# The first of three additions of a pair's weight sums, by accumulating transfers on GpSimd's queue

## The reference

```python
x = x + 0.5 * swiglu(rmsnorm(x, ffn1_norm), ffn1_w_gate, ffn1_w_up, ffn1_w_down)   # hidden width 5632
u = rmsnorm(x, mix_norm) @ w_in                                                     # 2048 x 6144
a = differential attention (4 heads) ; b = stick-breaking attention (8 heads)
x = x + concat(a, b) @ w_out
x = x + 0.5 * swiglu(rmsnorm(x, ffn2_norm), ffn2_w_gate, ffn2_w_up, ffn2_w_down)
x = rmsnorm(x, final_norm)

def swiglu(x, w_gate, w_up, w_down):
    return (silu(x @ w_gate) * (x @ w_up)) @ w_down
```

## Time and profile before

| | us |
|---|---|
| median of 3 runs | 1814.16 (1814.14 to 1814.62) |
| span of the profiled execution | 1811.7 |
| TensorE matmuls busy (8296) | 1800.1, 99% of the span |
| VectorE busy (1715 instructions) | 1415.1, 78% |
| ScalarE busy | 963.3, 53% |
| GpSimd busy | 21.7, 1% |
| HBM read | 346.85 MB, 193 GB/s over the span |

### The profile page before, as it was taken

One profiled execution on the slowest core, in us unless ns is written; L12 is line 12 of the kernel. 1 busy time (PEld: TensorE's weight loads), 2 busy tenths in 40 slices (PEclk: granted clock), 3 DMA queues, 4 the chain that ended last, 5 costly groups with the idle time before them and its releaser, 6 DMA issues.

```text
span 1811.7 us, 22258 instructions
## 1 busy us (share of the span) xinstructions
PE 1800.1 (99%) x8296; PEld 1498.7 (83%) x8296; DVE 1415.1 (78%) x1715; ACT 963.3 (53%) x1210; POOL 21.7 (1%) x19
## 2 busy tenths in 40 slices
PE   9999999999999999999999999999999999999998
PEld 7888888888888888888888888888888888888887
DVE  7889888889898868666666566889888887678865
ACT  7555445555454545555656455555455555345554
POOL 0000000000000000100000000000000000000000
PEclk9999999999999999999999999999999999999999
DMA  9565655556666657655465466665655557566653
GB/s 338 202 218 200 215 192 193 200 199 201 215 212 225 223 172 243 197 174 171 154 195 162 159 225 223 201 219 197 218 188 194 202 197 259 189 204 225 219 171 114
DMA packets 234116, 367.02 MB, mean 203 GB/s; under 512 B 16560, under 2 KB 95152, under 8 KB 234032
## 3 DMA queue, kind: packets, MB, share of 16 engines
q1 hardware_dynamic: 233120, 364.44, 59.4%
q10 hardware_dynamic: 912, 1.48, 0.2%
HBM read 346.85 MB, written 2.10 MB: 193 GB/s over the span
## 4 chain that ended last, share of the span: by engine, by line
PE 99%; DVE 0%; issue 0%; POOL 0%; DVEq 0%; ACT 0%
PE psum L1934 72%; PE psum L1975 14%; PE psum L1847 7%; PE psum L1852 3%; PE psum L1956 1%; PE psum L1808 0%; PE psum L2124 0%; PE psum L2135 0%; PE psum L2150 0%; PE psum L2170 0%; DVE x_res L1796 0%; PE psum L1814 0%; PE psum L1812 0%; PE psum L1813 0%; PE psum L1906 0%; PE psum L2183 0%
## 5 line engine op out<-in xcount | busy, mean ns | idle before, releaser
L1934 PE MATMUL psum<-w_split,x_split 128*128 128x512 f32 x3792 | 872.9, 390 | 0.0
L1934 PEld LDWEIGHTS psum<-w_split,x_split 128*128 128x128 f32 x3792 | 710.0, 188 | 149.7 <-DVE w_split L1252 1.4
L755 ACT ACTIVATE w_split<-w_raw 128x1024 fp32r<-128x1024 f32 (+1 forms) x520 | 517.9, 1013 | 458.2 <-PE psum L1934 325.8
L1252 DVE TENSOR_TENSOR w_split<-w_raw,w_split 128x1024 fp32r<-128x1024 f32 (+1 forms) x520 | 586.2, 1163 | 95.1 <-ACT w_split L755 89.7
L1934 PE MATMUL psum<-w_split,h_split 128*128 128x512 f32 x1920 | 439.2, 389 | 0.0
L1934 PEld LDWEIGHTS psum<-w_split,h_split 128*128 128x128 f32 x1920 | 359.8, 188 | 75.7 <-DVE w_split L1252 1.4
L1102 DVE TENSOR_TENSOR w_split<-w_raw,w_split 128x1024 fp32r<-128x1024 f32 (+1 forms) x244 | 284.0, 1190 | 94.1 <-ACT w_split L643 92.4
L643 ACT ACTIVATE w_split<-w_raw 128x1024 fp32r<-128x1024 f32 (+1 forms) x244 | 247.1, 1032 | 207.4 <-PE psum L1934 158.4
L1975 PE MATMUL psum<-w_split,pair_sums 128*128 128x512 f32 x624 | 162.6, 389 | 0.0
L1975 PEld LDWEIGHTS psum<-w_split,pair_sums 128*128 128x128 f32 x624 | 117.1, 188 | 24.3
L1975 PE MATMUL psum<-w_split,x_split 128*128 128x512 f32 x360 | 94.7, 389 | 0.0
(11 more groups left out here) (240 smaller groups left out, 1051.0 us busy)
## 6 DMA issues: line engine op xcount, KB each, us to landing
w_raw<-in_ffn_up SPq DMA_DIRECT2D x67, 1024.0 KB, 5.4
w_raw<-in_ffn_gate SPq DMA_DIRECT2D x66, 1024.0 KB, 8.0
w_raw<-in_ffn_down SPq DMA_DIRECT2D x64, 1024.0 KB, 5.7
w_raw<-in_w_in SPq DMA_DIRECT2D x48, 512.0 KB, 4.8
w_raw<-in_w_in SPq DMA_DIRECT2D x24, 1024.0 KB, 5.3
w_raw<-in_ffn_gate SPq DMA_DIRECT2D x42, 512.0 KB, 5.8
w_raw<-in_ffn_up SPq DMA_DIRECT2D x40, 512.0 KB, 6.2
w_raw<-in_w_out SPq DMA_DIRECT2D x16, 1024.0 KB, 5.1
```

Of the source, the lines that this page charges most:

```text
L755: nc.scalar.activation(w_split[:, n % 2, 0, part[0]:part[1]], w_raw[:, slot, part[0]:part[1]], ACT.Copy).then_inc(hi_made, 1)
L1252: nc.vector.tensor_tensor(w_split[:, n % 2, 1, part], w_raw[:, slot, part], w_split[:, n % 2, 0, part].bitcast(F32), ALU.subtract).then_in ...
L1934: ins = mm(psum[:, bank + t, :], x[:, a, t * P:(t + 1) * P], w[:, b, k, :], start=kk == from_ and (a, b) == (0, 0) and t in begins, stop=k ...
```

## The change

VectorE's first add of each pair (L1260, 128x1024) is dropped. In its place GpSimd's queue issues, as soon as the low part of the pair's block job is made, one DMA transfer with `accum_op=ALU.add` of 512 KB: it reads the second matrix's two blocks once more from HBM and adds them to b0 and b2 in the slot. b0 becomes the same sum as before, and so does b2. `sum_blocks` waits for that transfer (`block_sums[m]`) and makes the two remaining adds. It is called one step later: for m = 0 in step 1, behind job 3's low part; for m = 1 in step 3, behind job 5's. The transfers of all 26 groups, 52 in number, stand in GpSimd's program behind the first norm's power (`phases` up to the mix) and behind the second feed-forward part's (the rest).

```diff
--- before.py
+++ after.py
@@ -285,6 +285,7 @@
         half_used = sem("half_used")
         blocks_landed = [sem(f"blocks_landed{n}") for n in range(2)]
         weight_sums = sem("weight_sums")
+        block_sums = [sem(f"block_sums{n}") for n in range(2)]
         pair_step = sem("pair_step")
         pair_hi = sem("pair_hi")
         pair_ready = sem("pair_ready")
@@ -383,7 +384,7 @@
         seven_base = lambda ph, i: 2 * ph["s0"] - 2 * ph["plain"] + 10 * i
         seven_count = lambda ph, i: ph["sevens"] + i - ph["plain"]
         seven_steps = lambda ph, i: 6 * (ph["gates"] + i - ph["plain"])
-        weight_sums_value = lambda ph, i, m: 6 * seven_count(ph, i) + 3 * m
+        weight_sums_value = lambda ph, i, m: 4 * seven_count(ph, i) + 2 * m
         freed_steps = lambda ph: (2, 2, 2, 2) if ph["chunks"] == 4 else (1, 2, 1, 2)
         freed_value = lambda s: FREED_CREDIT + s + 1
         copied_value = lambda s: s - mix_s0 + 1
@@ -605,7 +606,29 @@
                 pool.wait_ge(norm_mean, n + 1)
                 power(rstd_tok[:, :], mean_sq[:, 0:2], norm_power)
 
+            def add_blocks(ph, i):
+
+                source = weights_of(ph)
+                for m in range(2):
+                    if ph["kind"] == "seven_wide":
+                        second = source(2 * i + 1, 0)[:, 2 * m:2 * m + 2, :]
+                    else:
+                        k = SEVEN_PAIRS[m] % 4
+                        second = source(i, 7)[:, k:k + 2, :]
+                    b = w_raw[:, 2 + m, :].rearrange("p (q n) -> p q n", n=2 * STRIP)
+                    pool.wait_ge(lo_made, lo_value(seven_base(ph, i) + 2 + m))
+                    nc.gpsimd.dma_start(b[:, 0:4:2, :], second, accum_op=ALU.add).then_inc(block_sums[m], 16)
+
+            def add_all_blocks(some):
+                for ph in some:
+                    jobs_before["extra"] = ph["extra"]
+                    if ph["kind"] in ("ffn_in", "seven_wide"):
+                        for i in range(ph["plain"], ph["bodies"] if ph["kind"] == "ffn_in" else 2):
+                            add_blocks(ph, i)
+
             norm_rstd(0)
+            mix_at = next(n for n, ph in enumerate(phases) if ph["kind"] == "mix")
+            add_all_blocks(phases[:mix_at])
             norm_rstd(NORM_MIX)
 
             def qk_power(n):
@@ -623,6 +646,7 @@
                 qk_power(n)
             out_power(1)
             norm_rstd(NORM_FFN2)
+            add_all_blocks(phases[mix_at:])
             norm_rstd(NORM_FINAL)
             pool.wait_ge(x_hi_made, 8 * NORM_FINAL + NS)
             pool.wait_ge(norm_ready, 2)
@@ -742,7 +766,7 @@
                 kind, raw = SEVEN_JOBS[n]
                 c, slot = seven_base(ph, i) + n, raw % 4
                 if kind == "sums":
-                    act.wait_ge(weight_sums, weight_sums_value(ph, i, raw - 2) + 3)
+                    act.wait_ge(weight_sums, weight_sums_value(ph, i, raw - 2) + 2)
                 else:
                     act.wait_ge(landed[slot], 16 * (ph["s0"] // 2 + 2 * i + raw // 4 + 1))
                 if kind == "blocks":
@@ -1256,11 +1280,9 @@
 
                 b = w_raw[:, 2 + m, :].rearrange("p (q n) -> p q n", n=2 * STRIP)
                 done = weight_sums_value(ph, i, m)
-                dve.wait_ge(lo_made, lo_value(seven_base(ph, i) + 2 + m))
-                nc.vector.tensor_tensor(b[:, 0:4:2, :], b[:, 0:4:3, :], b[:, 2:3, :].broadcast_to([P, 2, 2 * STRIP]), ALU.add).then_inc(weight_sums, 1)
+                dve.wait_ge(block_sums[m], 16 * (seven_count(ph, i) + 1))
+                nc.vector.tensor_tensor(b[:, 3, :], b[:, 0, :], b[:, 3, :], ALU.add).then_inc(weight_sums, 1)
                 dve.wait_ge(weight_sums, done + 1)
-                nc.vector.tensor_tensor(b[:, 3, :], b[:, 0, :], b[:, 3, :], ALU.add).then_inc(weight_sums, 1)
-                dve.wait_ge(weight_sums, done + 2)
                 nc.vector.tensor_tensor(b[:, 1, :], b[:, 3, :], b[:, 1, :], ALU.add).then_inc(weight_sums, 1)
 
             def seven_gates(ph, i):
@@ -1306,7 +1328,7 @@
                             seven_hidden(ph, i)
                             turn_blocks(s)
                     seven_low(ph, i, n + 2, ph["next_kn"] if at_end and n >= 8 else ph["kn"])
-                    if n in (0, 2):
+                    if n in (1, 3):
                         sum_blocks(ph, i, n // 2)
                     if n == 6:
                         seven_gates(ph, i)
```

## The result

The changed kernel takes 1881.25 us in the median of 4 runs (1878.65 to 1882.04), against 1814.17 before: ratio 1.0368, 95% interval 1.0355 to 1.0381. It is 67 us slower. The forecast was 1861 in a range of 1819 to 1895: the right side, and some 20 us short. The profiled execution has a span of 1879.0 us, 67.3 more than before.

The account below looks back on a forecast made before the run. TensorE, busy for 99% of the span, was taken as the bound. A stall beyond cover of 41.4 us plus 5.2 for the order made 46.6, on a span of 1811.7: 1858.3, as a run 1861, range 1819 to 1895.

Parts of the forecast that it names:

- The bound and the sign: TensorE, busy for 99% of the span, bounds the kernel; slower by over 0.2% was given 0.91.
- point 5: VectorE's wait for m=0's transfer behind job 3's low half holds up job 4's low halves: 41.4 us.
- L: Length of the 512 KB accumulating transfer: 6.0 us, ends 3.7 and 9.7; each us is worth 26 us.
- The cover: From job 2's low half's end to VectorE reaching m=0's wait: 4.2 to 4.3 us in 14 of 26 groups.
- point 2: m=0's two adds behind job 3's low half make job 4 late by 0.2 us a group, 5.2 us.
- C: Rival: VectorE's two-input instructions hold back the transfer on GpSimd's queue, L 7.2 or more, 1892 us; chance 0.21.
- Point 3: m=1's adds behind job 5's low half have about 1 us to spare before job 6: costed at nothing.
- point 4: The 52 added transfers on GpSimd's free queue cost nothing by bandwidth; DMA engines busy 0.20 and 0.17 there.
- B: Rival: transfer hidden before job 4, L up to 4.2; only the order's loss and short covers remain, 1819.4 us; chance 0.12.
- D: Rival: handover into job 4 loses nothing, 0.3 us of old gap gained, 1813.9 us; chance 0.07 same, 0.02 faster.

Follow-up runs that it names:

- experiment 4: The changed kernel with both pairs' sums later still (m=0 behind job 4's low halves, m=1 between job 5's): 1830.83 us with the transfers, 1830.33 without.
- experiment 5: The changed kernel with only m=1 by transfer, m=0's three adds on VectorE behind job 2's low half: 1824.64 us; its complement is m=0 alone.
- experiment 1: The changed kernel without its 52 transfers, first addition left out, the two other adds at the change's places: 1816.33 us.
- m=0 alone: The changed kernel with only m=0 by transfer, m=1's three adds on VectorE behind job 4's low halves: 1880.6 us.
- experiments 1 to 4 and 6: Besides experiment 1 and experiment 4, against the changed kernel: plain copies on GpSimd's queue 1831.36 us, ScalarE's 1827.53; transfers halved 1828.25; three adds on VectorE, new places 1857.77.
- experiment 7: The changed kernel with 8 matmuls of no use between jobs 3 and 4, in TensorE's gap: 1873.15 us.

## Why the prediction was right, and where it was short

- **The bound and the sign** (point 5, the new wait). Right, and shown: without the transfers 1816, with the transfers but no wait for them nothing is added (experiment 4), with a wait for half of each 1828, with the whole wait 1881. The gap is where the forecast put it, before job 4 and in all 26 groups.
- **L.** Forecast 6.0 us, counted from the end of the low half; measured 6.42 in the mean: 26 x 0.42 = 11 us more. The row from which I took it, a 1 MB load, gives nearly the right number for a reason that the runs bear out: an accumulating transfer moves at about half the bytes a second (208 against 408 GB/s). No row shows the reading of its target by itself. What I left out is the 0.3 us between the low half's end and GpSimd's issue row.
- **The cover.** 4.2, 5.4 and 3.6 us by class, 4.43 in the mean after the change and 4.41 before. It is the part of the sum that held best.
- **The order's 0.2 us a group** (point 2): 0.13 measured, behind job 4's first matmul and not before the job; 5.2 us forecast, some 3 found, 0.9 of them there before the change.
- **The step that failed is one that isn't in the sum**: what TensorE's clock does after the idle time. I summed the gaps as if TensorE came back at full speed. In seven groups it ran at a granted clock of 0.5 for 3.4 us, 11 us lost in all, and 8 matmuls of no use took the spells away. With L's 11 us more and the order's 2 less: 46.6 + 11 + 11 - 2 = 67. That the time still fell in the range owes something to the range's width, which was set for C and not for the clock.
- **Point 3** (m=1 is free). True in the change, where m=0's wait makes the cover 6.6 us or more. Without that wait it isn't shown. In experiment 5 m=0's adds don't stand behind job 3's low half, so the cover is 4.7 to 5.8 us and not the forecast's 6, and m=1 alone costs 11 us, nearly all of it in the four groups with 4.7.
- **"DMA has room"** (point 4). The engines are fully busy while an accumulating transfer runs (1.11 in the row above), not at a fifth; but nobody waited for what they held up (0.5 us between the two runs of experiment 4), so that costing it at nothing was right in effect.
- **Rivals.** B (hidden) would have needed 4.2 us, which a plain copy (4.5) or half a transfer (4.3) nearly has. C's mechanism, an issue held back by VectorE, isn't there: GpSimd's issue takes 1.2 us in all 52 cases (1194 to 1358 ns). In many of them VectorE is idle beside it, but where it subtracts for 1.16 of the 1.20 us (at 283 us) the row is 1203 ns, the same as beside an idle VectorE (at 237). D is out: without the transfers (experiment 1) the 0.3 us of old gap did go, and nothing else.

No version with transfers reached the kernel before. None could gain much: TensorE's gaps in the 26 groups came to 1.2 us in all before the change.

## What to carry to other kernels

When an operation is moved from an engine to a transfer, what counts is the time from the last write of the data to the landing, less the work that lies between, on the engine that waits in order: 6.4 us against 4.4 here, times 26. If the transfer is longer than its cover, split it so that the in-order engine waits only for the part that it reads (1881 to 1828 us by this alone). And when a change makes TensorE idle for a couple of microseconds at a time, look at the granted clock behind each gap: here 3.4 us at 0.5 behind seven of the 26 gaps cost 11 us on top of them.

## What the runs showed of the hardware

- An accumulating transfer of 512 KB from memory to SBUF landed in 6.1 to 6.2 us (medians), a plain one on the same queue in 4.5 and on ScalarE's in 4.1; 256 KB accumulating in 4.3. The DMA engines read as fully busy at 208 GB/s, against 408 for a plain load; a 2 KB packet took 178 ns on GpSimd's queue, accumulating, against 84 on SyncE's.
- GpSimd's issue took 1.20 us for an accumulating 512 KB and 0.72 for a plain one; for two accumulating pieces of 256 KB back to back, 0.87 and 1.22.
- After idle times of 1.99 to 3.61 us TensorE's granted clock fell to 0.5 for 3.4 us (once 6.8) in 7 of the 26 groups of the changed kernel, in 8 with m=0 alone and in 14 with the delayed issue; in these groups it never fell where all gaps were 1.4 us or less (experiments 1 to 4 and 6), nor with single ones of 1.81 (experiment 7) and 2.26 (experiment 5, m=1 alone).
- One program's matmuls ran at 0.2334 us a piece throughout, and not 0.2267, with the same matmuls, at full granted clock and on two chips. What it had beyond the others was a small operation on GpSimd, which had not run yet when the pace was already slow, and an 8-byte tile ahead of the weight slots. No run moved the tile. Not settled.
